# The recurrence's triangles inverted by 32x32 blocks, and attention units spread over its steps

## The chip, the core and the metric

One core of a Trainium2 chip runs the whole kernel. The metric is the time of one execution on the device, in microseconds. The core has a matrix engine (TensorE, PE below; its weight loads are listed apart as PEld), VectorE (DVE), ScalarE (ACT), GpSimd (POOL) and SyncE (SP), which issues DMAs. Every engine runs its own list of instructions in order and waits for the others on semaphores. The lists are fetched from memory by DMA; their packets have a queue of their own in the profile.

## The reference

One step of a decoder layer, for a prompt of 512 tokens and 8 sampled sequences of 8 tokens each with a past of 1,024 cached keys: project the normed input, mix it in four groups of four heads (RWKV7, FoX, MoBA, stick-breaking), project back, then a normed MLP. The part that changes is the RWKV7 recurrence:

```python
def step(s, inp):
    r_t, w_t, k_t, v_t, kk_t, a_t = inp
    sa = jnp.einsum('bhij,bhj->bhi', s, -kk_t)
    s = (s * w_t[:, :, None, :] + sa[..., None] * (kk_t * a_t)[:, :, None, :]
         + v_t[..., None] * k_t[:, :, None, :])
    return s, jnp.einsum('bhij,bhj->bhi', s, r_t)
...
s_fin, y = lax.scan(step, s0.astype(f32), xs)
```

The other three groups are softmax or stick-breaking attention over the prompt (24 attention units here, with the prompt's own keys) and over the cached keys.

## The kernel before

The 576 new tokens (512 of the prompt, 64 sampled) are cut into nine chunks of 64. Inside a chunk the recurrence is solved at once: with L the strictly lower triangular 64x64 matrix of products of kk and kk a, the kernel needs the inverse of (1 + L) for each chunk and head. It builds it by doubling: X starts as the inverse of the diagonal's 2x2 blocks, and level lev (0 to 4) joins neighbouring blocks of size 2, 4, 8, 16 and 32: W = (L masked to this level) X, dX = X W, X = X - dX. The transpose XT (slot 8) goes along through dXT. All this is done with full 64x64 products.

The recurrence is a list STEPS of (kind, a), a = 0 or 1 for a pair of heads: LT and L (both triangles), ArbT, LkT, ArkT, Vt, KQt, BEt, KEt, then W, dX, dXT by level, then T1, HT, H, G, MT, N, seq1 to seq7 (the state from chunk to chunk), U, Y, SS, GM, GV. They are numbered R0 to R74. Each of LT to G is 18 products of 64x64 (nine chunks, two heads on the two halves of the partitions), all issued from line 1154 in `per_chunk`. A product in fp32 is two matmul instructions, each with its weight load, so a step is 36 loads and 36 matmuls. The result stands in PSUM, 128 partitions by 576 columns, in one of two buffers used in turn; `begin` has TensorE wait until the step two back is evicted, and until its operands are there. ScalarE evicts the kinds in BY_ACT (`take_product`, line 1908), VectorE the others (`rwkv_steps`, lines 2507 to 2537, with a mask multiplied or a subtraction done on the way).

What stands between two steps is written out by hand in PLAN: TensorE, ScalarE and VectorE all walk the same list ORDER. In it As u, Ap u and Ay u are the three parts of attention unit u on TensorE (scores, lines 1277; probabilities turned, line 1294; times V, line 1303), with the softmax or stick-breaking work on the other engines between them; units 0 to 5 cover the first 128 queries and 128 keys, 6 to 11 the second 128 queries and 256 keys, and so on. The piece with number u of As, Ap and Ay runs the stage of unit u, u-2 and u-2. K u turns and scores cached keys (lines 1317, 1325 and 1339: 128x128 turns, then products with 32-column weights on four parts of the array in turn), V u multiplies cached values, G ends the recurrence, L loads forget gates. Before R23 the steps follow each other, with L at L_AT.

rc holds masks (lines 60 to 110 of the constants), loaded by two DMAs on SyncE's queue: first part in_rc 16, second in_rc 32. GpSimd stores the new keys and values (kv) during the steps.

Of the kernel before, what the change touches and what calls it, by code (L numbers as in the profile page):

```python
# [33 lines left out]
T = SEQ + NS  # L34
# [8 lines left out]
CH = 64  # L43
# [23 lines left out]
R_SU, R_IU, R_LEV, R_L1, R_L1T, R_BM = 0, 576, 1152, 1472, 1536, 1600  # L67
# [11 lines left out]
def constants():  # L79
# [17 lines left out]
    for n, m in enumerate((2, 4, 8, 16, 32)):  # L97
        rc[:, R_LEV + n * 64:R_LEV + (n + 1) * 64] = level(t[None, :], q[:, None], m)
    rc[:, R_L1:R_L1 + 64] = level(q[:, None], t[None, :], 1)
    rc[:, R_L1T:R_L1T + 64] = level(t[None, :], q[:, None], 1)  # L100
# [20 lines left out]
def build(nc, d, o):  # L121

    ctx = ExitStack()
    with ctx:
# [63 lines left out]
        def chunked(n):  # L188
            return slot(n).rearrange("p a (c s) -> p a c s", s=CH)

# [176 lines left out]
        ltm_ready = sem("ltm_ready")  # L367
        masked_ready = sem("masked_ready")
# [290 lines left out]
        BY_ACT.update({f"W{lev}": (5, 1.0) for lev in range(5)})  # L659

# [35 lines left out]
        L_AT = (2, 6, 10)  # L696
        AFTER = {n: [("L", L_AT.index(n))] for n in L_AT}
        ORDER = []
        for n in range(A_FROM):
            ORDER += [("R", n)] + AFTER.get(n, [])  # L700
        PLAN = """
            As0 R23 R24 R25 Ap0 Ay0 As1 R26 R27 Ap1 R28 R29 Ay1 As2 R30 R31 R32 R33 R34 R35 R36 R37 R38 Ap2 Ay2 R39
            R40 As3 R41 R42 Ap3 R43 R44 Ay3 R45 R46 As4 R47 R48 Ap4 R49 Ay4 As5 R50 R51 R52 R53 R54 R55 R56 R57 Ap5
            R58 R59 R60 R61 R62 R63 R64 Ay5 As6 R65 Ap6 Ay6 As7 B0 R66 Ap7 R67 R68 B1 Ay7 R69 R70 As8 R71 R72 Ap8
            As9 Ay8 R73 R74 G0 G1 Ap9 G2 K0 G3 K1 G4 Ay9 K2 As10 K3 Ap10 K4 Ay10 As11 K5 Ap11 K6 Ay11 K7 As12 K8
            Ap12 K9 K10 K11 Ay12 K12 K13 As13 K14 Ap13 K15 Ay13 As14 K16 K17 K18 Ap14 K19 Ay14 K20 K21 K22 As15 K23
            K24 N0 S0 Ap15 Ay15 P0 M0 K25 As16 K26 K27 Ap16 K28 Ay16 Q0 K29 K30 X0 As17 K31
            Ap17 K32 Ay17 K33 X1 As18 K34 Ap18 K35 Ay18 X2 K36 As19 V0 K37 K38 V1 Ap19 K39 Ay19 K40 As20 K41 V2 V3 Ap20 K42 Ay20 As21 V4 K43
            Ap21 K44 V5 Ay21 K45 K46 As22 V6 K47 N1 Ap22 V7 Ay22 S1 As23 V8 Ap23 V9 Ay23 P1 As24 Ap24 F0 O0 T0 M1 X3
            Ay24 As25 Q1 Ap25 O1 X4 X5 Ay25 O2 V10 O3 V11 V12 V13 V14 V15 V16 V17 V18 V19 F1 T1  # L710
# [231 lines left out]
        def _(pe):  # L942
# [217 lines left out]

            def rwkv_products():

                for kind, A, B in (("LT", 8, 1), ("L", 1, 8), ("ArbT", 8, 4), ("LkT", 3, 1), ("ArkT", 3, 4),
                                   ("Vt", 6, eye), ("KQt", 1, eye), ("BEt", 9, eye), ("KEt", 5, eye)):
# [525 lines left out]
        def _(act):  # L1690
# [166 lines left out]
            for t in range(4):  # L1857
                take(5, t)
            act.wait_ge(logf_in, 1)
            nc.scalar.preload_act_table_set("natural_log_exp_and_others")  # L1860
# [346 lines left out]
        def _(dve):  # L2207
# [291 lines left out]
            id64 = cst[:, K_ID64:K_ID64 + 64].unsqueeze(1).to_broadcast([128, NCH, 64])  # L2499
            def rwkv_steps():  # L2500

                for kind, dst, m in (("LT", 0, R_SU), ("L", 2, None), ("ArbT", 11, R_IU), ("LkT", 7, R_SU), ("ArkT", 12, R_IU)):
                    for a in range(2):
                        src = take(kind, a)
                        if kind == "L":
                            dve.wait_ge(in_rc, 32)
                            link(tt(chunked(dst)[:, a], r3(src), mask64(R_L1), MUL))
                            tt(chunked(dst)[:, a], id64, chunked(dst)[:, a], SUB).then_inc(c_ev, 1)  # L2508
                            yield
                        else:  # L2510
                            tt(slot(dst)[:, a, :], src, rc[:, m:m + T], MUL).then_inc(c_ev, 1)
                            yield
                def level_mask(lev, a):
                    tt(chunked(3)[:, a], chunked(0)[:, a], mask64(R_LEV + 64 * lev), MUL).then_inc(ltm_ready, 1)

                for kind, dst in (("Vt", 14), ("KQt", 15), ("BEt", 17), ("KEt", 18)):
                    for a in range(2):
                        if kind in ("Vt", "KQt"):
                            if kind == "Vt":
                                link(tt(chunked(8)[:, a], chunked(0)[:, a], mask64(R_L1T), MUL))  # L2520
                                link(tt(chunked(8)[:, a], id64, chunked(8)[:, a], SUB))
                            else:
                                level_mask(0, a)
                        yield
                dve.wait_ge(c_ev, AT["KEt", 1] + 1 - by_act(AT["KEt", 1] + 1))
                for lev in range(5):
                    for a in range(2):
                        if lev < 4:
# [692 lines left out]
```

## Time and profile before

| | us |
|---|---|
| median of three runs | 936.02 (933.02 to 936.2) |
| span of the profiled execution | 930.9 |
| time around the span (median less span) | 5.1 |
| first recurrence product (R0) | 205.8 |
| HT (R48) starts | 267.3 |
| sequential state steps start, end | 283.7, 290.7 |
| K0 starts | about 320 |
| As12 (behind K7) starts | 339.8 |

The span is that of one execution taken by the hardware profiler; the times of the runs are of unprofiled ones. The profiled execution has no time of its own apart from the span; its time is taken as the median, so 5.1 us lie around the span. The rows give microseconds, counted from the span's start, unless marked ns.

### The profile page before, as it was taken

How to read it: one execution, taken by the hardware profiler on the slowest of the kernel's cores; microseconds unless marked ns; L12 is line 12 of the kernel's file. 1: busy time of each engine (PE TensorE's matmuls, PEld its weight loads, DVE VectorE, ACT ScalarE, POOL GpSimd, SP SyncE). 2: the span in 40 equal slices, each digit the busy share in tenths (PEclk: the TensorE clock that was granted, in tenths of full speed). 3: DMA queues.
4: the chain of work that ended last, by engine and by line, in shares of the span. 5: the costliest groups of instructions: out<-in, count | busy, mean ns of one | idle time of the engine just before them, and what ended most of it. 6: DMA issues, size and time to landing. Idle time of an engine off the chain costs nothing.

```text
span 930.9 us, 21268 instructions
## 1 busy us (share of the span) xinstructions
PE 894.3 (96%) x8588; PEld 769.5 (83%) x8588; DVE 640.8 (69%) x1083; ACT 452.0 (49%) x771; POOL 63.0 (7%) x95
## 2 busy tenths in 40 slices
PE   6999999998999999979999999999999999999998
PEld 5999899998887667756655789978998899889986
DVE  5563377647756763665664662789988988988796
ACT  6422636313241466775562533453574456535751
POOL 0000112114500000000000000100110000000000
PEclk9999999999999999989999999999999999999999
DMA  8542787861200687648997704886889532443343
GB/s 270 181 137 69 160 203 198 241 133 62 83 6 3 216 283 241 221 141 282 305 397 259 246 20 137 206 271 183 244 211 258 191 91 93 179 136 92 132 143 144
DMA packets 73163, 164.47 MB, mean 177 GB/s; under 512 B 5918, under 2 KB 32126, under 8 KB 70890
## 3 DMA queue, kind: packets, MB, share of 16 engines
q1 hardware_dynamic: 59370, 124.26, 38.9%
q0 software_dynamic: 13696, 38.85, 17.9%
q8 instruction: 68, 1.11, 0.5%
q14 instruction: 29, 0.24, 0.1%
HBM read 156.55 MB, written 40.10 MB: 211 GB/s over the span
## 4 chain that ended last, share of the span: by engine, by line
PE 82%; DVE 11%; ACT 3%; DMA 2%; issue 2%; DVEq 0%; ACTq 0%; SPq 0%
PE PS L962 16%; PE PS L964 15%; PE PS L963 15%; PE PS L1154 7%; PE PS L1317 4%; PE PS L1389 2%; PE PS L1339 2%; PE PS L995 2%; PE PS L1277 2%; PE PS L1303 2%; PE PS L1425 2%; DVE WL L2924 1%; PE PS L1294 1%; PE PS L1629 1%; PE PS L1630 1%
## 5 line engine op out<-in xcount | busy, mean ns | idle before, releaser
L963 PE MATMUL PS<-WL,U 128*128 128x512 f32 x224 | 87.6, 391 | 0.0
L962 PE MATMUL PS<-WH,U 128*128 128x512 f32 x224 | 87.5, 390 | 0.0
L2037 ACT ACTIVATE WH<-Wraw 128x1024 fp32r<-128x1024 f32 x56 | 57.9, 1056 | 48.9 <-PE PS L964 19.9
L2924 DVE TENSOR_TENSOR WL<-Wraw,WH 128x1024 fp32r<-128x1024 f32 x56 | 66.9, 1219 | 7.9 <-ACT WH L2037 7.9
L1154 PE MATMUL PS<-AR 64*64 64x64 f32 x1912 | 61.6, 219 | 4.0 <-DVE AR L2508 1.4
L1154 PEld LDWEIGHTS PS<-AR 64*64 64x64 f32 x1912 | 58.5, 135 | 7.3 <-issue 4.2
L962 PE MATMUL PS<-WR,HR 128*128 128x384 f32 (+1 forms) x184 | 63.7, 346 | 0.8 <-issue 0.8
L962 PE MATMUL PS<-h2H,WH 128*128 128x288 f32 x208 | 61.4, 295 | 1.2 <-DVE rc L3046 1.2
L1317 PE MATMUL PS<-cst,AR 128*128 128x128 f32 x384 | 54.7, 286 | 7.6 <-ACT W L1915 7.6
L963 PE MATMUL PS<-h2L,WH 128*128 128x288 f32 x208 | 61.2, 294 | 0.0
L964 PE MATMUL PS<-h2H,WL 128*128 128x288 f32 x208 | 61.2, 294 | 0.0
L1317 PEld LDWEIGHTS PS<-cst,AR 128*128 128x128 f32 x384 | 43.3, 145 | 20.5 <-ACT W L1915 10.7
L964 PE MATMUL PS<-WH,U 128*128 128x512 f32 x152 | 59.2, 389 | 0.0
L962 PE MATMUL PS<-TF,WH 128*128 128x288 f32 x192 | 56.8, 296 | 0.0
L963 PE MATMUL PS<-TF,WH 128*128 128x288 f32 x192 | 56.7, 295 | 0.0
L964 PE MATMUL PS<-TF,WL 128*128 128x288 f32 x192 | 56.5, 294 | 0.0
L963 PE MATMUL PS<-WR,HR 128*128 128x384 f32 (+1 forms) x160 | 53.9, 337 | 0.0
L1915 ACT ACTIVATE W<-PS 128x512 f32<-128x512 f32 x72 | 40.0, 594 | 25.7 <-PE PS L1317 25.7
L962 PEld LDWEIGHTS PS<-WH,U 128*128 128x128 f32 x224 | 42.1, 188 | 9.4 <-DVE VQ L3050 0.4
L963 PEld LDWEIGHTS PS<-WL,U 128*128 128x128 f32 x224 | 42.0, 188 | 9.0
L964 PE MATMUL PS<-WR,VQL 128*128 128x384 f32 (+1 forms) x138 | 46.3, 335 | 0.0
L2097 ACT ACTIVATE WH<-Wraw 128x1024 fp32r<-128x1024 f32 x24 | 25.4, 1060 | 31.4 <-DVE Wraw L2990 16.2
(436 smaller groups left out, 2310.4 us busy)
## 6 DMA issues: line engine op xcount, KB each, us to landing
AR<-in_cache_kv SPq DMA_DIRECT2D x120, 384.0 KB, 4.8
tau<-in_w_mlp_down POOLq DMA_DIRECT2D x24, 1024.0 KB, 9.0
Wraw<-tau SPq DMA_DIRECT2D x16, 1024.0 KB, 4.8
Wraw<-in_w_mlp_up SPq DMA_DIRECT2D x14, 1024.0 KB, 5.6
Wraw<-in_w_mlp_down SPq DMA_DIRECT2D x12, 1024.0 KB, 5.1
W<-in_w_in SPq DMA_DIRECT2D x6, 1536.0 KB, 9.6
QK<-in_cache_kv SPq DMA_DIRECT2D x8, 384.0 KB, 5.4
AR<-in_x_prompt SPq DMA_DIRECT2D x4, 512.0 KB, 6.8
```

The source lines that it names most:

```text
L962: mm(out, lH, rH, start=start, stop=False, skip_group_check=skip)
L963: mm(out, lH, rL, start=False, stop=False, skip_group_check=skip)
L964: return mm(out, lL, rH, start=False, stop=stop, skip_group_check=skip)
L995: last = mm(PS[rows, bank:bank + c1 - c0], hs[k // 6][:, k % 6, :], piece_raw(i)[:, k, c0:c1], start=(k == 0), stop=(k == KT - 1), skip_gr ...
L1154: last = mm(PS[h, base + c * CH:base + (c + 1) * CH], chunked(A)[h, a, c, :], B(h, a, c) if callable(B) else chunked(B)[h, a, c, :], start ...
L1277: last = mm(PS[:, (4 + h) * 512:(4 + h) * 512 + nk], qT[rows, j, qt * 128:(qt + 1) * 128], kT[rows, j, 0:nk], start=True, stop=True)
L1303: last = mm(PS[64 * h:64 * h + 64, turned_at(u) * 512:turned_at(u) * 512 + 128], V(k, (2 * j + h) * HD, HD), PTp[:, h, k * 128:(k + 1) * 1 ...
L1317: last = turn(PS[:, bank * 512 + bb * 128:bank * 512 + (bb + 1) * 128], page_home("K", s)[:, bb, (m % 6) * 128:(m % 6 + 1) * 128], ident)
L1915: f(KTr[m % 4], PS[:, KEY_BANK[m] * 512:(KEY_BANK[m] + 1) * 512], ACT.Copy).then_inc(kt_ev, 1)
L2037: f(piece_half(WH, r, d, h), piece_half(Wraw, r, d, h), ACT.Copy).then_inc(w_hi, 1)
L2097: ins = f(form_pair(WH, p, r), raw_pair(i, p), ACT.Copy)
L2924: tt(piece_half(WL, r, d, h), piece_half(Wraw, r, d, h), piece_half(WH, r, d, h).bitcast(F32), SUB).then_inc(w_lo, 1)
```

## The change

Each triangle of 64x64 is treated as two diagonal 32x32 blocks and one crossing block. LT and L are computed by halves: only the diagonal blocks, 32 columns each, and for LT the crossing block in 32x32 pieces. Levels 0 to 3 act on the diagonal blocks alone, as 32x32x32 products on the four diagonal tiles of the array in turn (`per_block`); levels 2 and 3 leave out the ninth chunk (the sampled tokens, in groups of 8). Level 4 becomes W4 and dXT4, 16 products each on the crossing block, with T1 between them. The blocks lie in halves of the slots (`blocks`); VectorE puts the diagonal blocks of XT into slot 8 by eight copies, and ScalarE adds the crossing one. Evictions are 288 or 256 columns wide. Half-size PSUM buffers let `begin` look three steps back instead of two within the levels. LT is evicted by ScalarE in three pieces. Masks move within rc, so that L needs the first part alone. L_AT changes, an activation table is preloaded a little earlier, and the list of items is new up to K8: there are as many steps as before, but the units stand elsewhere. From K8 on the list is the same.

```diff
         STEPS = [(k, a) for k in ("LT", "L", "ArbT", "LkT", "ArkT", "Vt", "KQt", "BEt", "KEt") for a in (0, 1)]
-        for lev in range(5):
-            STEPS += [(f"{k}{lev}", a) for k in (("W", "dX", "dXT") if lev < 4 else ("W", "dXT")) for a in (0, 1)]
-        STEPS += [(k, a) for k in ("T1", "HT", "H", "G", "MT", "N") for a in (0, 1)]
+        for lev in range(4):
+            STEPS += [(f"{k}{lev}", a) for k in ("W", "dX", "dXT") for a in (0, 1)]
+        STEPS += [(k, a) for k in ("W4", "T1", "dXT4", "HT", "H", "G", "MT", "N") for a in (0, 1)]
...
+        BY_ACT.update({"LT": (0, 1.0), "dXT4": (8, -1.0)})
+        HALVED = [f"{k}{lev}" for lev in range(4) for k in ("W", "dX", "dXT")]
+        def level_chunks(lev):
+            return NCH if lev < 2 else NCH - 1
+        def step_at(n):
+            return (n % 2) * 1024 + (n // 2 % 2 * 512 if STEPS[n][0] in HALVED else 0)
+        def step_out(n, chunks=NCH):
+            return PS[:, step_at(n):step_at(n) + chunks * HC].rearrange("p (c s) -> p c s", s=HC)
+        def before_step(n):
+            return n - 3 if all(m < len(STEPS) and STEPS[m][0] in HALVED for m in (n, n - 2, n - 4)) else n - 1
...
-        L_AT = (2, 6, 10)
+        L_AT = (1, 6, 10)
...
         PLAN = """
-            As0 R23 R24 R25 Ap0 Ay0 As1 R26 R27 Ap1 R28 R29 Ay1 As2 R30 R31 R32 R33 R34 R35 R36 R37 R38 Ap2 Ay2 R39
-            R40 As3 R41 R42 Ap3 R43 R44 Ay3 R45 R46 As4 R47 R48 Ap4 R49 Ay4 As5 R50 R51 R52 R53 R54 R55 R56 R57 Ap5
-            R58 R59 R60 R61 R62 R63 R64 Ay5 As6 R65 Ap6 Ay6 As7 B0 R66 Ap7 R67 R68 B1 Ay7 R69 R70 As8 R71 R72 Ap8
-            As9 Ay8 R73 R74 G0 G1 Ap9 G2 K0 G3 K1 G4 Ay9 K2 As10 K3 Ap10 K4 Ay10 As11 K5 Ap11 K6 Ay11 K7 As12 K8
...
+            As0 R23 Ap0 R24 Ay0 R25 As1 R26 Ap1 R27 R28 Ay1 R29 As2 R30 Ap2 R31 R32 Ay2 R33 As3 R34 Ap3 R35 Ay3 R36
+            R37 As4 R38 Ap4 R39 Ay4 R40 R41 As5 R42 Ap5 R43 Ay5 R44 As6 R45 R46 Ap6 R47 Ay6 R48 As7 R49 R50 Ap7 R51
+            Ay7 R52 As8 R53 Ap8 R54 R55 As9 R56 Ay8 R57 Ap9 R58 R59 R60 R61 R62 R63 R64 R65 B0 R66 Ay9 R67 As10 R68 B1
+            Ap10 R69 Ay10 R70 R71 As11 R72 Ap11 R73 Ay11 R74 G0 G1 G2 K0 G3 K1 G4 K2 K3 K4 K5 K6 K7 As12 K8 Ap12 K9
...
-                need = max([AT[x, a] + 1 for x in after] + ([n - 1] if n >= 2 else []), default=0)
+                need = max([AT[x, a] + 1 for x in after] + ([before_step(n)] if n >= 2 else []), default=0)
                 evacuated(pe, need)
-                return (n % 2) * 1024
+                return step_at(n)
...
+            def halves_of(base, a, A, B):
+                for c in range(NCH):
+                    for h in (0, 64):
+                        for b in (0, HC):
+                            last = mm(PS[h + b:h + b + HC, base + c * HC:base + (c + 1) * HC],
+                                      chunked(A)[h:h + 64, a, c, b:b + HC], chunked(B)[h:h + 64, a, c, b:b + HC],
+                                      start=True, stop=True)
+                return last
+            def per_block(base, a, A, B, chunks):
+                for c in range(chunks):
+                    for r in range(0, 128, HC):
+                        last = mm(PS[r:r + HC, base + c * HC:base + (c + 1) * HC], A[r:r + HC, a, c, :], B[r:r + HC, a, c, :],
+                                  start=True, stop=True)
+                return last
...
+                LTm, X, XT, W_ = blocks(3), blocks(2), blocks(2, True), blocks(5)
+                for lev in range(4):
+                    chunks = level_chunks(lev)
                     for a in range(2):
                         base = begin(f"W{lev}", a, "L" if lev == 0 else f"dX{lev - 1}", "KEt")
                         pe.wait_ge(ltm_ready, 2 * lev + a + 1)
-                        per_chunk(base, a, 3, 2).then_inc(c_ps, 1)
+                        per_block(base, a, LTm, X, chunks).then_inc(c_ps, 1)
                         yield
-                    if lev < 4:
-                        for a in range(2):
-                            base = begin(f"dX{lev}", a, f"W{lev}")
-                            per_chunk(base, a, 8, 5).then_inc(c_ps, 1)
-                            yield
+                    for a in range(2):
+                        base = begin(f"dX{lev}", a, f"W{lev}")
+                        per_block(base, a, XT, W_, chunks).then_inc(c_ps, 1)
+                        yield
                     for a in range(2):
                         base = begin(f"dXT{lev}", a, f"W{lev}")
-                        per_chunk(base, a, 5, 8).then_inc(c_ps, 1)
+                        per_block(base, a, W_, XT, chunks).then_inc(c_ps, 1)
                         yield
-                for kind, A, B, after in (("T1", 7, 14, ()), ("HT", 15, 8, ("dXT4",)), ("H", 8, 15, ()), ("G", 8, 9, ("T1",))):
+                for a in range(2):
+                    base = begin("W4", a, "dX3")
+                    for c in range(NCH - 1):
+                        for h in (0, 64):
+                            last = mm(PS[h + HC:h + CH, base + c * HC:base + (c + 1) * HC], blocks(0, True)[h:h + HC, a, c, :],
+                                      X[h:h + HC, a, c, :], start=True, stop=True)
+                    last.then_inc(c_ps, 1)
+                    yield
...
+                for a in range(2):
+                    base = begin("dXT4", a, "W4", "dXT3")
+                    for c in range(NCH - 1):
+                        for h in (0, 64):
+                            last = mm(PS[h:h + HC, base + c * HC:base + (c + 1) * HC], W_[h + HC:h + CH, a, c, :],
+                                      XT[h + HC:h + CH, a, c, :], start=True, stop=True)
+                    last.then_inc(c_ps, 1)
+                    yield
+                for kind, A, B, after in (("HT", 15, 8, ("dXT4",)), ("H", 8, 15, ()), ("G", 8, 9, ("T1",))):
                     for a in range(2):
                         base = begin(kind, a, *after)
+                        if kind == "HT":
+                            pe.wait_ge(xt_ready, a + 1)
                         per_chunk(base, a, A, B).then_inc(c_ps, 1)
...
+                    elif kind == "LT":
+                        f(blocks(0)[:, a], step_out(n), ACT.Copy)
+                        crossing = PS[:, step_at(n) + 512:step_at(n) + 512 + (NCH - 1) * HC].rearrange("p (c s) -> p c s", s=HC)
+                        f(blocks(0, True)[0:HC, a, 0:NCH - 1], crossing[0:HC], ACT.Copy)
+                        f(blocks(0, True)[CH:CH + HC, a, 0:NCH - 1], crossing[CH:CH + HC], ACT.Copy).then_inc(x_ev, 1)
+                    elif kind == "W4":
+                        f(blocks(5)[HC:CH, a, 0:NCH - 1], step_out(n, NCH - 1)[HC:CH], ACT.Copy)
+                        f(blocks(5)[CH + HC:128, a, 0:NCH - 1], step_out(n, NCH - 1)[CH + HC:128], ACT.Copy).then_inc(x_ev, 1)
+                    elif kind == "dXT4":
+                        f(chunked(8)[0:HC, a, 0:NCH - 1, HC:CH], step_out(n, NCH - 1)[0:HC], ACT.Copy, scale=scale)
+                        f(chunked(8)[CH:CH + HC, a, 0:NCH - 1, HC:CH], step_out(n, NCH - 1)[CH:CH + HC], ACT.Copy,
+                          scale=scale).then_inc(x_ev, 1)
+                    elif kind in HALVED:
+                        chunks = level_chunks(int(kind[1:]))
+                        f(blocks(dst)[:, a, 0:chunks], step_out(n, chunks), ACT.Copy, scale=scale).then_inc(x_ev, 1)
...
+                for a in range(2):
+                    dve.wait_ge(c_ps, AT["L", a] + 1)
+                    link(tt(X[:, a], step_out(AT["L", a]), mask32(R_L1), MUL))
+                    tt(X[:, a], mask32(R_ID), X[:, a], SUB).then_inc(c_ev, 1)
+                    yield
...
-                for lev in range(5):
+                for lev in range(4):
+                    chunks = level_chunks(lev)
                     for a in range(2):
-                        if lev < 4:
+                        if lev < 3:
                             dve.wait_ge(c_ps, AT[f"W{lev}", a] + 1)
                             level_mask(lev + 1, a)
                         yield
-                    for k, x in ((("dX", 2), ("dXT", 8)) if lev < 4 else (("dXT", 8),)):
+                    for k, x in (("dX", X), ("dXT", XT)):
                         for a in range(2):
-                            src = take(f"{k}{lev}", a)
-                            if x == 8 and lev < 4 or x == 2:
-                                dve.wait_ge(c_ps, AT[f"dXT{lev}", a] + 1 if x == 8 else AT[f"dX{lev}", a] + 1)
-                            tt(slot(x)[:, a, :], slot(x)[:, a, :], src, SUB).then_inc(c_ev, 1)
+                            n = AT[f"{k}{lev}", a]
+                            dve.wait_ge(c_ps, n + 1)
+                            tt(x[:, a, 0:chunks], x[:, a, 0:chunks], step_out(n, chunks), SUB).then_inc(c_ev, 1)
                             yield
-                dve.wait_ge(c_ev, AT["dXT4", 1] + 1 - by_act(AT["dXT4", 1] + 1))
-                for kind in ("T1", "HT", "H", "G"):
+                dve.wait_ge(c_ev, AT["dXT3", 1] + 1 - by_act(AT["dXT3", 1] + 1))
+                for a in range(2):
+                    for r in range(0, 128, HC):
+                        ins = copy(chunked(8)[r:r + HC, a, :, r % CH:r % CH + HC], XT[r:r + HC, a])
+                    ins.then_inc(xt_ready, 1)
+                    yield
```

## Rows read from the trace of the kernel before

**Rows 1.** The page, first lines: engines' busy us (share), instructions.

```profile
span 930.9 us, 21268 instructions
PE 894.3 (96%) x8588; PEld 769.5 (83%) x8588; DVE 640.8 (69%) x1083; ACT 452.0 (49%) x771; POOL 63.0 (7%) x95
```

**Rows 2.** Windows: length, PE, PEld, DVE, ACT, POOL busy (count), PE clock, DMA, GB/s.

```profile
205.80:267.32 61.52, 56.80 (x1731) 53.72 (x1731) 41.63 (x85) 17.25 (x38) 24.43 (x44) 1.00 0.24 74
319.53:339.77 20.24, 17.74 (x227) 13.44 (x227) 16.75 (x37) 15.86 (x34) 1.11 (x2) 1.00 0.60 213
...
205.80:233.88 28.08, 25.21 (x804) 24.32 (x805) 19.27 (x31) 8.23 (x13) 12.04 (x24) 1.00 0.29 90
...
233.88:252.02 18.14, 16.71 (x505) 15.86 (x505) 13.18 (x33) 4.45 (x12) 12.39 (x21) 1.00 0.33 101
```

**Rows 3.** Groups by line and shape, 205 to 320: busy us, mean ns.

```profile
L1908 ACT ACTIVATE AR<-PS 128x576 f32<-128x576 f32 x22 | 14.3, 650 | 46.3 <-PE PS L1154 46.2
L2537 DVE TENSOR_TENSOR AR<-AR,PS 128x576 f32<-128x576 f32 x18 | 13.6, 756 | 9.0 <-PE PS L1154 8.9
...
L2642 DVE TENSOR_TENSOR W<-PS,VQ 128x256 f32<-128x256 f32 x2 | 0.8, 425 | 0.0
```

**Rows 4.** Chain of waits, two recurrence steps: start, us, engine, line.

```profile
256.83 2.24 PE PS L1154 x72
```

**Rows 5.** Timeline of PE: start, length until the last one's end, count.

```profile
302.14 0.75 PE L1233 MATMUL PS<-AR,VQ 64*64 64x8 f32 x11
...
327.42 0.30 PE L1339 MATMUL PS<-W,rc 128*32 128x128 f32 x1
...
327.42 0.32 PE L1339 MATMUL PS<-W,rc 128*32 128x128 f32 x4
```

**Rows 6.** The page, DMA queue of instructions: packets, MB, share of 16 engines.

```profile
q8 instruction: 68, 1.11, 0.5%
```

**Rows 7.** Chain of waits: the two gaps called issue.

```profile
233.50 0.39 issue
...
250.98 1.04 issue
```

**Rows 8.** DMA, windows 231.72:232.70, 249.76:250.72, 254.1:255.6, 257.89:261.33, in order.

```profile
q8 instruction: 1, 0.02, 6.0%
...
q0 software_dynamic: 86, 0.28, 85.7%
q8 instruction: 1, 0.02, 6.1%
...
q8 instruction: 1, 0.02, 4.9%
...
q8 instruction: 2, 0.03, 4.2%
```

**Rows 9.** Chain of waits: pieces of units, first 128 queries, then second.

```profile
259.07 0.42 PE PS L1277 x4
...
264.35 0.37 PE PS L1303 x4
...
315.25 0.44 PE PS L1294 x4
315.69 0.63 PE PS L1277 x4
316.32 0.61 PE PS L1303 x8
```

**Rows 10.** DMA, window 207.0:209.7: the masks' load.

```profile
q1 hardware_dynamic: 357, 0.94, 93.9%
```

**Rows 11.** Chain of waits: cached keys turned and scored.

```profile
324.23 1.02 PE PS L1317 x8
325.26 0.57 PE PS L1339 x16
```

**Rows 12.** Windows: a gap among the cached keys, and behind it.

```profile
336.64:338.38 1.74, 0.00 (x1) 0.00 (x0) 1.44 (x3) 1.71 (x5) 0.00 (x0) 1.00 0.97 369
340.08:343.49 3.41, 3.41 (x24) 2.04 (x24) 2.15 (x8) 1.00 (x2) 0.00 (x0) 0.50 0.90 295
```

More of the change, by code:

```diff
@@ L96, in level @@
         return (a // (2 * m) == b // (2 * m)) & (a // m % 2 == 1) & (b // m % 2 == 0)
[L97 to L100, printed above, removed]
+    w, j = p % HC, np.arange(HC)
+    for n, m in enumerate((2, 4, 8, 16)):
+        rc[:, R_LEV + n * HC:R_LEV + (n + 1) * HC] = level(j[None, :], w[:, None], m)
+    rc[:, R_L1:R_L1 + HC] = level(w[:, None], j[None, :], 1)
+    rc[:, R_L1T:R_L1T + HC] = level(j[None, :], w[:, None], 1)
+    rc[:, R_ID:R_ID + HC] = (w[:, None] == j[None, :])
     for b in range(DB):
@@ L189, in chunked, with blocks @@
             return slot(n).rearrange("p a (c s) -> p a c s", s=CH)
+        def blocks(n, second=False):
+            return slot(n)[:, :, T // 2 * second:T // 2 * (second + 1)].rearrange("p a (c s) -> p a c s", s=HC)
         ARf = AR[:, :, :].rearrange("p a c -> p (a c)")
@@ L1159, in eye @@
                 return cst[h, K_ID:K_ID + 128][:, h]
-            def rwkv_products():
-                for kind, A, B in (("LT", 8, 1), ("L", 1, 8), ("ArbT", 8, 4), ("LkT", 3, 1), ("ArkT", 3, 4),
+            def halves_of(base, a, A, B):
[12 more added lines that the diff above has]
+                return last
+            def rwkv_products():
+                for a in range(2):
+                    base = begin("LT", a)
+                    halves_of(base, a, 8, 1)
+                    for c in range(NCH - 1):
+                        for h in (0, 64):
+                            last = mm(PS[h:h + HC, base + 512 + c * HC:base + 512 + (c + 1) * HC],
+                                      chunked(8)[h:h + 64, a, c, 0:HC], chunked(1)[h:h + 64, a, c, HC:CH], start=True, stop=True)
+                    last.then_inc(c_ps, 1)
+                    yield
+                for a in range(2):
+                    base = begin("L", a)
+                    halves_of(base, a, 1, 8).then_inc(c_ps, 1)
+                    yield
+                for kind, A, B in (("ArbT", 8, 4), ("LkT", 3, 1), ("ArkT", 3, 4),
                                    ("Vt", 6, eye), ("KQt", 1, eye), ("BEt", 9, eye), ("KEt", 5, eye)):
@@ new lines, in rwkv_products @@
+                for a in range(2):
+                    base = begin("T1", a)
+                    per_chunk(base, a, 7, 14).then_inc(c_ps, 1)
+                    yield
+                for a in range(2):
+                    base = begin("dXT4", a, "W4", "dXT3")
+                    for c in range(NCH - 1):
+                        for h in (0, 64):
+                            last = mm(PS[h:h + HC, base + c * HC:base + (c + 1) * HC], W_[h + HC:h + CH, a, c, :],
+                                      XT[h + HC:h + CH, a, c, :], start=True, stop=True)
+                    last.then_inc(c_ps, 1)
+                    yield
@@ L2497, in mask64, with mask32 @@
                 return rc[:, c0:c0 + 64].unsqueeze(1).to_broadcast([128, n, 64])
-            id64 = cst[:, K_ID64:K_ID64 + 64].unsqueeze(1).to_broadcast([128, NCH, 64])
+            def mask32(c0, n=NCH):
+                return rc[:, c0:c0 + HC].unsqueeze(1).to_broadcast([128, n, HC])
             def rwkv_steps():
-                for kind, dst, m in (("LT", 0, R_SU), ("L", 2, None), ("ArbT", 11, R_IU), ("LkT", 7, R_SU), ("ArkT", 12, R_IU)):
+                X, XT = blocks(2), blocks(2, True)
+                for a in range(2):
+                    yield
+                for a in range(2):
+                    dve.wait_ge(c_ps, AT["L", a] + 1)
+                    link(tt(X[:, a], step_out(AT["L", a]), mask32(R_L1), MUL))
+                    tt(X[:, a], mask32(R_ID), X[:, a], SUB).then_inc(c_ev, 1)
+                    yield
+                for kind, dst, m in (("ArbT", 11, R_IU), ("LkT", 7, R_SU), ("ArkT", 12, R_IU)):
@@ L2503, in rwkv_steps @@
                     for a in range(2):
                         src = take(kind, a)
-                        if kind == "L":
+                        if (kind, a) == ("ArbT", 0):
                             dve.wait_ge(in_rc, 32)
[L2507 to L2512, printed above, removed]
+                        tt(slot(dst)[:, a, :], src, rc[:, m:m + T], MUL).then_inc(c_ev, 1)
@@ L2513, in level_mask @@
+                        yield
                 def level_mask(lev, a):
-                    tt(chunked(3)[:, a], chunked(0)[:, a], mask64(R_LEV + 64 * lev), MUL).then_inc(ltm_ready, 1)
-                for kind, dst in (("Vt", 14), ("KQt", 15), ("BEt", 17), ("KEt", 18)):
+                    chunks = level_chunks(lev)
+                    tt(blocks(3)[:, a, 0:chunks], blocks(0)[:, a, 0:chunks], mask32(R_LEV + HC * lev, chunks),
+                       MUL).then_inc(ltm_ready, 1)
+                for kind in ("Vt", "KQt", "BEt", "KEt"):
@@ L2517, in rwkv_steps @@
                     for a in range(2):
[L2518 to L2523, printed above, removed]
+                        if kind == "Vt":
+                            evacuated(dve, AT["LT", a] + 1)
+                            link(tt(XT[:, a], blocks(0)[:, a], mask32(R_L1T), MUL))
+                            link(tt(XT[:, a], mask32(R_ID), XT[:, a], SUB))
+                        elif kind == "KQt":
+                            level_mask(0, a)
+                        elif kind == "BEt":
+                            link(nc.vector.memset(chunked(8)[:, a, :, 0:HC], 0.0))
+                            link(nc.vector.memset(chunked(8)[:, a, NCH - 1, HC:CH], 0.0))
@@ L2524, in rwkv_steps @@
                         yield
                 dve.wait_ge(c_ev, AT["KEt", 1] + 1 - by_act(AT["KEt", 1] + 1))
-                for lev in range(5):
+                for lev in range(4):
+                    chunks = level_chunks(lev)
                     for a in range(2):
-                        if lev < 4:
+                        if lev < 3:
                             dve.wait_ge(c_ps, AT[f"W{lev}", a] + 1)
```

22 lines of the change are left out of this document (15 added, 7 removed).

## Prediction

> **What bounds the kernel now.** I read the page first for what is busy: TensorE 96% of the span [rows 1], and in the chain that ended last nearly all pieces are its own. So a change is priced on TensorE's own list, and what VectorE and ScalarE save counts only where TensorE waits for them. Second, the table by stage [rows 2]: from the start of the recurrence's products (205.80) to its step HT (267.32) TensorE is busy 56.80 of 61.52 us, so at most 4.72 us of waiting can be filled there; in 319.53 to 339.77, where the first cached keys are turned, 17.74 of 20.24. Third, the groups by line, for the price of an eviction: a product of 576 columns costs ScalarE 650 ns and VectorE 756, one of 256 columns 425 [rows 3].
>
> Fourth, what one small matmul costs. A step of 18 products 64x64 is 36 matmul records, each with its weight load; two such steps, 72 records, take 2.24 us with their start [rows 4], 29.2 ns per load and matmul in the steady run. Two things about that pace matter. Matmuls of 8 columns on one 64x64 tile in a row run 11 in 0.75 us [rows 5], up to 68 ns each, whereas two tiles in turn with 64 columns make two in 58. So a small product is set by how quickly one tile can follow itself, hardly by its columns. And where four 32-column tiles are in turn, four matmuls lie inside 0.32 us where one alone takes 0.30 [rows 5]: they start some 7 ns apart. Bursts may start that close; what a long run can keep up is another question.
>
> Fifth, the instruction queue, which decides that. The page has 68 packets on it [rows 6], against 2 x 8,588 matmuls and loads [rows 1]: some 253 instructions per packet of 16 KB (I read: pages of 256). TensorE has two gaps put down to "issue", 0.39 us at 233.50 and 1.04 at 250.98 [rows 7]. Between their ends lie 505 matmuls and 505 loads [rows 2], four pages less the semaphore instructions that the row doesn't count. Just ahead of each gap's end an instruction packet moved: at 231.73, 6.0% of 16 engines over 0.98 us, so 0.94 us long, and at 249.77, beside queue 0's kv stores [rows 8]. Both gaps end 1.2 to 1.3 us after the packet. So TensorE ran out of instructions twice, and with only one page in hand, for a packet late by a microsecond or two was enough. The next packet started 1.4 us after the first gap and 2.2 after the second, at 254.19 [rows 8]. Round of one page when starved: 1.4 + 0.9 + 1.2 = 3.5 us in quiet, 2.2 + 1.2 + 1.2 = 4.6 beside other transfers. The shortest spacing of two packets in the whole trace is 3.42 us, in the window of 3.44 that holds two [rows 8]. I take 3.4 us per 256 instructions, 26.6 ns per load and matmul. At 29.2 ns a page lasts 3.74 us: today the fetch is just hidden.
>
> The Trainium skill speaks against this: Runtime: NRT & Kernel Launch, section Instruction fetch mechanics, says that the sequencer fetches the next 16 KiB block while it works on the current one, so that fetching is hidden, because dispatch is slower than the fill. The two gaps disagree, at a pace of 14.6 ns per instruction. By the rule the sum would have no fetch term and come out as the second rival below.
>
> **The change part by part.**
>
> *More, smaller instructions.* Counted from the diff: 32 steps of 36 pairs of load and matmul (LT, L, levels 0 to 4) = 1,152 pairs become LT 2 x 104, L 2 x 72, levels 0 and 1 twelve steps of 72, levels 2 and 3 twelve of 64, W4 and dXT4 four of 32 = 2,112. That is 960 pairs or 1,920 instructions more, 7.5 pages.
>
> *Units moved ahead of HT.* Before R48 stand two more As, three more Ap and three more Ay: 138 instructions. By the pieces in the chain (As 0.42, or 0.63 from unit 6 on; Ay 0.37, and Ap taken like it [rows 9]) 3.3 us, and 8 x 0.14 us for changing over from the recurrence's matmuls (an estimate from the same 2.24 us: 72 x 29.2 ns is 2.10) = 4.4 us.
>
> *When HT starts.* From 205.80 to HT there are 3,462 matmuls and loads [rows 2]; with 1,920 + 138 and about 1% semaphores, 5,570. Counting pages back from the gap at 233.50 (1,609 instructions after 205.80, twelve semaphores, five pages: 341), the first 341 are at hand; the page after them comes with the packet at 209.74, which waits behind the masks' load, when queue 1 keeps the engines 94% busy [rows 10], and is usable at 211.9. What is left, 5,230 instructions, is 20.4 pages x 3.4 = 69.4 us; three of them late at 4.6 instead of 3.4 (the two late ones above and one more in the kv stores) give 3.5. HT at 211.9 + 69.4 + 3.5 = 284.8 instead of 267.3: **+17.5**. The moved units hide in those waits, and so do the evictions at half width, whose cover is the same fetch; without it they'd be bound by 0.45 us per step, under the 1.05 of a step now.
>
> Bounds of this term: if the fetch never binds, and a pair still costs one tile 58 ns, four tiles in turn make it 14.6; the steps take 1,984 x 14.6 + 128 x 29.2 = 32.7 us against 33.6, and with the units' 4.4 and 1.5 for the page at 211.9 HT moves by +5.0. If a round is 2.5 us instead of 3.4 (below the shortest spacing seen, not excluded, since no page was ever asked for faster), 20.4 x 0.9 = 18 us fall away and that bound holds as well. At the other end 29.2 ns per pair as today: 2,112 x 29.2 = 61.7, +28.1.
>
> *Small things.* LT's eviction goes to ScalarE in three pieces (about 1.3 us a step), LT is off VectorE, L no longer waits for the second half of the masks, eight small copies and T1 stand between W4 and HT: all ScalarE or VectorE work of under 2 us per step, covered by the fetch; if that cover is gone, T1's 1.05 us covers the copies. I take 0, at most +1.
>
> *HT to the end of the recurrence's chain* (R48 on): eight pieces instead of four; 4.1 us against 1.5 by the pieces' prices, the second 128 queries' Ap at 0.44 and Ay at 0.61 [rows 9], + 4 x 0.14, less little waiting filled: **+3.0**.
>
> *R65 to R74*: seven pieces, 4.0 us, instead of eleven, 5.4, and 4 x 0.14 less: **-2.0**.
>
> *K0 to K7*: no pieces instead of eight. Without one, a K takes 1.02 + 0.57 [rows 11], some with 0.2 more: 8 x 1.70 = 13.6 us in place of 20.24. The gap of 1.74 us with TensorE idle at 336.64 goes too, and I expect that the 3.41 us at half the clock after it [rows 12] go, worth 1.7: 20.24 + 1.7 - 13.6 = **-8.3** (-6.6 if the clock falls elsewhere). From K8 on the lists agree: nothing.
>
> **Sum.** The profiled execution's span is 930.9; the median of the runs is 936.0, so 5.1 lie around it. 936.0 + 17.5 + 3.0 - 2.0 - 8.3 = 946.2: **946 us**. Its own range, with rounds of 3.0 to 3.7 us (-8, +6) and the clock, is 938 to 955.
>
> **Rivals.**
>
> *No fetch limit, four blocks overlap at 14.6 ns per pair.* 936.0 + 5.0 + 3.0 - 2.0 - 8.3 = 933.7, about no change. For it: pages have never been asked for faster, so the round may overlap; against it the two gaps. 18%.
>
> *The blocks cost half as much again, faster.* If 32 rows halve a tile's round, a pair costs 7.3 ns, the steps 16 us instead of 33.6; the evictions and the page at 211.9 then bind, HT moves by about -6, and the whole is 936.0 - 6 + 3.0 - 2.0 - 8.3 = 923. For it: the starts 7 ns apart [rows 5]. Against: up to 68 ns for 8 columns. It decides if a round of the fetch is below 2.0 us. 10%.
>
> *Every instruction keeps today's 14.6 ns*, whichever tile it goes to: HT +28.1, sum 936.0 + 28.1 + 3.0 - 2.0 - 8.3 = 957; with a page late here and there 959. For it: no longer run in the trace is faster than today's products; against it only short bursts. The Trainium skill has a rule of this kind (TensorE: Matmul & The Clock Gate, section Wait — 56ns, not 53.3ns?: start to start not under about 25 ns however few the columns); by it 2,112 matmuls would take at least 53 us, an estimate, and the sum would be 948. The four starts in 0.32 us disagree with it for different tiles. 13%.
>
> *The fetch limits, and TensorE, idle in each page, drops to its lower clock* (1.2 GHz) as it did after the gap at 336.64 [rows 12]: with a quarter of the 51 us from HT to K8 at half the clock, 946 + 51/8 = 952. 7%.
>
> **Chances.** Forecast 52%, the rivals as above. Faster by over 0.5% (under 931.3; half a per cent is about what a measurement of this kernel can tell): the second rival 10, a third of the first 6, a tail of the forecast 4: 20%. Within: 17%. Slower: 63%. The range runs from 926 (leaves out the second rival and a little) to 960.
>
> **What would show it.** Right: the instruction queue has 75 to 76 packets; in the level steps the matmuls come in bursts of some 250 instructions with starts a few ns apart, and gaps of 1 to 2 us called "issue", each ending 1.2 us after an instruction packet; packets 3.4 to 3.5 us apart from W0 to dXT4; HT near 285, the first K near 338, K8 some 13.6 us later. Wrong: level steps of 1.05 us without such gaps (then 934), or of 0.5 (923); evenly spaced pairs of 29 ns would be the third rival. The prediction fails if pages can be had faster than 3.4 us when asked for, which no row of before tests.

## The result, and the profile after

The changed kernel takes 961.44 us (median of four runs, 961.01 to 963.42) against 936.11 (933.02 to 936.55): ratio 1.0278, 95% interval 1.026 to 1.0297. It is slower, as forecast, but by 25 us and not by 10, and just outside the stated range. The first lines of its page, the granted clock in 40 slices, the instruction queue and the costliest new group, in answer to [rows 1] and [rows 6]:

```profile
span 960.0 us, 23197 instructions
PE 903.8 (94%) x9548; PEld 773.6 (81%) x9548; DVE 631.5 (66%) x1089; ACT 453.4 (47%) x783; POOL 61.9 (6%) x95
...
PEclk9999999998558989999999999999999999999999
...
q8 instruction: 76, 1.25, 0.5%
...
L1201 PE MATMUL PS<-AR 32*32 32x32 f32 x1632 | 27.3, 235 | 18.0 <-issue 18.0
```

960 more matmuls and as many loads, eight more instruction packets, and 18.0 us of "issue" ahead of the 32x32 products, a kind of idle time of which the kernel before has 1.4 us in its products. Two more gaps, 5.0 us together, stand ahead of products of LT and L. In the chain of waits, these two and then the first of the levels, which start at 236.2:

```profile
207.94 3.84 issue
...
214.62 1.16 issue
...
236.23 0.72 PE PS L1201 x52
236.95 2.85 issue
239.80 2.01 PE PS L1201 x126
241.80 1.70 issue
243.50 1.92 PE PS L1201 x127
245.42 1.77 issue
```

The gaps end multiples of 256 apart in TensorE's list (within one instruction): counted from its start, with semaphore instructions, they end ahead of instructions 3,009, 3,265, 4,545, 4,801, 5,057, 5,314 and so on, the two of [rows 7] at 4,289 and 5,313. Between two of the gaps shown stand 126 or 127 matmuls with their loads, one page, done in 2 us; the rest of the time TensorE has none. The windows by stage (columns as in [rows 2]): from R0 to W0, to T1, to HT, to the first sequential step, to As12:

```profile
206.07:236.16 30.09, 23.77 (x862) 22.69 (x863) 12.89 (x29) 8.11 (x16) 12.70 (x26) 0.83 0.23 70
236.16:291.99 55.83, 37.84 (x1746) 31.43 (x1744) 21.28 (x72) 11.49 (x40) 11.61 (x19) 0.52 0.15 44
291.99:299.48 7.49, 7.15 (x148) 5.82 (x147) 6.90 (x22) 4.36 (x13) 0.00 (x0) 0.69 0.02 4
299.48:317.47 17.99, 17.52 (x444) 15.07 (x442) 11.23 (x38) 9.57 (x27) 0.00 (x0) 1.00 0.01 3
317.47:371.72 54.25, 49.91 (x708) 37.73 (x709) 31.71 (x64) 18.28 (x36) 1.11 (x2) 0.94 0.42 139
```

The last column but two is the granted clock: 0.52 in the levels, so nearly all at the lower level (1.2 GHz), where the kernel before has 1.00 [rows 2]. Against the same stages of before:

| stage | before | after | difference |
|---|---|---|---|
| R0 to W0 | 23.00 | 30.09 | +7.1 |
| W0 to T1 | 36.94 | 55.83 | +18.9 |
| T1 to HT | 2.67 | 7.49 | +4.8 |
| HT to the sequential steps | 15.24 | 17.99 | +2.7 |
| sequential steps to As12 | 56.11 | 54.25 | -1.9 |
| As12 to the end | 591.1 | 588.3 | -2.8 |

T1 stands ahead of dXT4 in the changed kernel and behind it before, so the second and the third line are better read as one: 39.6 us before, 63.3 after, +23.7. Of the +7.1 in the first line, 5.0 are the two gaps ahead of LT and L.

One slip in what stands ahead: HT (R48) of the kernel before starts at 268.4; 267.3 is the second step of T1. The span grew by 29.1 us, the medians by 25.3. Around the span of after lie 1.7 us (961.7 of its own time less 960.0), and 1.6 to 1.8 in every execution of the other kernels that lists both, not the 5.1 that I added. So the execution profiled before took some 932.6 us (an estimate, 930.9 and 1.7): near the lowest of its times (933.02), not the median.

### The profile page after: what moved, and what is told of

It is laid out like the page before. It is cut to its first block, busy times and chain, and to the rows that moved or that the text cites. A ratio compares the mean times of both kernels' runs of the same rounds, so it can differ in the third digit from the quotient of the medians.

```text
span 960.0 us, 23197 instructions
## 1 busy us (share of the span) xinstructions
PE 903.8 (94%) x9548; PEld 773.6 (81%) x9548; DVE 631.5 (66%) x1089; ACT 453.4 (47%) x783; POOL 61.9 (6%) x95
## 4 chain that ended last, share of the span: by engine, by line
PE 82%; DVE 11%; issue 4%; ACT 2%; DMA 0%; DVEq 0%; ACTq 0%
PE PS L988 15%; PE PS L989 15%; PE PS L990 15%; PE PS L1180 4%; PE PS L1397 4%; PE PS L1201 3%; PE PS L1469 2%; PE PS L1419 2%; PE PS L1357 2%; PE PS L1021 2%; PE PS L1383 2%; DVE WL L3038 1%; PE PS L1505 1%; PE PS L1374 1%; PE PS L1710 1%
## 5 line engine op out<-in xcount | busy, mean ns | idle before, releaser
L988 PE MATMUL PS<-WH,U 128*128 128x512 f32 x224 | 87.7, 392 | 0.0
L1397 PE MATMUL PS<-cst,AR 128*128 128x128 f32 x384 | 54.7, 287 | 6.0 <-ACT W L2010 5.1
L1201 PE MATMUL PS<-AR 32*32 32x32 f32 x1632 | 27.3, 235 | 18.0 <-issue 18.0
L1201 PEld LDWEIGHTS PS<-AR 32*32 32x32 f32 x1632 | 24.2, 148 | 22.7 <-issue 20.3
L2192 ACT ACTIVATE WH<-Wraw 128x1024 fp32r<-128x1024 f32 x24 | 25.4, 1059 | 31.5 <-DVE Wraw L3104 21.6
```

What stands on the lines that cost most here:

```text
L988: mm(out, lH, rH, start=start, stop=False, skip_group_check=skip)
L1201: last = mm(PS[r:r + HC, base + c * HC:base + (c + 1) * HC], A[r:r + HC, a, c, :], B[r:r + HC, a, c, :], start=True, stop=True)
L1397: last = turn(PS[:, bank * 512 + bb * 128:bank * 512 + (bb + 1) * 128], page_home("K", s)[:, bb, (m % 6) * 128:(m % 6 + 1) * 128], ident)
L2192: ins = f(form_pair(WH, p, r), raw_pair(i, p), ACT.Copy)
```

## The experiments

Eleven runs were made, on two chips; each stands against the kernel before as it ran beside it (931.6 us on one chip, 933.1 and 934.0 on the other). The theory: pages of 256 instructions, at 3.4 us or more each, set TensorE's pace. Its rivals: the new list, the lower clock, the pace of small products.

**The list alone.** Old triangles, new list:

```diff
-        L_AT = (2, 6, 10)
+        L_AT = (1, 6, 10)
...
-            As0 R23 R24 R25 Ap0 Ay0 As1 R26 R27 Ap1 R28 R29 Ay1 As2 R30 R31 R32 R33 R34 R35 R36 R37 R38 Ap2 Ay2 R39
+            As0 R23 Ap0 R24 Ay0 R25 As1 R26 Ap1 R27 R28 Ay1 R29 As2 R30 Ap2 R31 R32 Ay2 R33 As3 R34 Ap3 R35 Ay3 R36
```

> The old triangles by 64x64 products with the new list of items and the new places of the forget-gate items. If the loss comes from the number of TensorE's instructions (fetch theory), the list alone costs nothing: HT moves by 0 to +4 us, the stretch behind it by -3 to -6, and the time is 929 to 937 us with TensorE at full clock throughout the recurrence. If the list is what costs (rival: the pieces between the steps delay the recurrence), it is 945 us or more.

Measured: 938.57 us, ratio 1.0073 (1.0049 to 1.0097): 7 us slower, between the two. HT comes 7.2 us later, where I had 0 to 4, and behind the sequential steps only 2.8 us come back up to As12. What takes it there is a wait that I had not priced. Its chain of waits:

```profile
324.92 0.76 DVE AR L2592
...
326.31 0.70 DVE W L2654
...
327.04 0.70 DVE W L2654
...
330.42 0.77 DVE AR L2592
...
331.24 1.24 PE PS L1251 x4
```

Between the group norm's two halves (L2592) VectorE does 4 us of a stick-breaking unit (the scans of L2654), since As11 now stands there in the list; TensorE's product L1251 waits 3.4 us for the second half. The changed kernel has the same wait; in this run and in that one, by the waits of TensorE:

```profile
PE PS L1251 <- DVE AR L2592: 3.4, 1, 3.4
```

```profile
PE PS L1331 <- DVE AR L2706: 3.3, 1, 3.3
```

**The blocks alone.** New triangles, old list from R23 on.

> The new triangles by 32x32 blocks with the old list (only the first forget-gate item stays at its new place). Fetch theory: still 960 to 967 us, since all 1,920 added instructions are there: gaps called issue at page boundaries, 256 instructions apart, 3.5 us or more from page to page, and the lower clock. Rival, the list costs: 940 us or less.

Measured: 960.1 us, ratio 1.0284 (1.0242 to 1.0327), HT at 296.9, 28.5 us later than before. The blocks carry the whole loss; the list's 7 us hardly add to them (HT at 299.5 with both, 2.6 us later and not 7.2). I take it that its pieces fill time in which TensorE has no instructions; no run shows that by itself.

**TensorE kept busy.** Two matmuls of 192 columns ahead of each step of LT, L and levels 0 to 3:

```diff
+            def keep_busy(base):
+                for _ in range(2):
+                    mm(PS[:, base + 304:base + 496], ident, cst[:, 0:192], start=True, stop=True)
...
             def per_block(base, a, A, B, chunks):
+                keep_busy(base)
```

> The changed kernel, with two matmuls of 128x128x192 that nobody reads put ahead of each of the 28 steps LT, L and levels 0 to 3, so that TensorE has work while it waits for its next page (some 220 instructions more). Fetch theory with the clock as a second cost: the clock stays high, pages still come 3.5 to 3.7 us apart, the time falls by 6 to 12 us to 950 to 955. If the lower clock is the main cost (rival), the time falls to 940 us or below. If the clock costs nothing, it rises by the added 3 us to 964.

Measured: 964.52 us, ratio 1.034 (1.0308 to 1.0372), as if the clock cost nothing, and not 950 to 955. W0 to T1 by windows, and a stretch of its timeline:

```profile
237.30:293.71 56.41, 47.90 (x1838) 38.04 (x1837) 20.74 (x71) 10.30 (x37) 11.24 (x18) 0.94 0.14 42
```

```profile
239.60 0.82 PE L1208 MATMUL PS<-AR 32*32 32x32 f32 x72
240.35 0.92 PE L1201 MATMUL PS<-cst 128*128 128x192 f32 x4
241.20 0.38 PE L1208 MATMUL PS<-AR 32*32 32x32 f32 x23
242.37 0.62 PE L1208 MATMUL PS<-AR 32*32 32x32 f32 x49 [0.79 <-issue]
```

The clock is 0.94 in place of 0.52, the stage as long, and the pages as far apart: 14 spacings in 54.7 us, 3.90 us each, against 13 in 51.0, 3.92, in the changed kernel. Its gaps called issue are shorter, 8.5 us in the stage and not 18.0, since the added matmuls stand in them, and the pages come no sooner. So in the starved levels the lower clock goes with TensorE's idle time and costs next to nothing of its own. Outside them it does cost: from ArbT to the end of KEt there are no gaps between pages and nothing was added, and that stretch is 2.4 us longer in the changed kernel, where a quarter of it ran at the lower clock (first row, granted clock 0.87), than here (second row, 1.00):

```profile
216.68:236.16 19.48, 18.34 (x515) 17.72 (x511) 11.66 (x25) 4.55 (x7) 8.32 (x18) 0.87 0.14 42
```

```profile
219.47:236.53 17.06, 16.02 (x519) 15.47 (x511) 11.67 (x25) 4.56 (x7) 7.27 (x15) 1.00 0.13 38
```

The timeline also gives the blocks' own price at full clock: the next group starts 0.75 us after a step of 72 pairs, 10 ns per pair.

**One pass.** The blocks' operands in bfloat16, half the instructions in the same steps:

```diff
-            return slot(n)[:, :, T // 2 * second:T // 2 * (second + 1)].rearrange("p a (c s) -> p a c s", s=HC)
+            return slot(n).bitcast(BF16)[:, :, T // 2 * second:T // 2 * (second + 1)].rearrange("p a (c s) -> p a c s", s=HC)
```

> The changed kernel with the blocks' operands kept in bfloat16, so that a block product is one load and one matmul instead of two of each; list, steps, tiles, waits and evictions stay. This changes the precision of the triangles' inverse. 880 pairs, 1,760 instructions, 6.9 pages fewer. Fetch theory: 6.9 pages x 3.7 us less and most of the lower clock gone: 926 to 938 us. Rivals: only TensorE's work counts, 880 x 7.8 ns = 7 us less, 954 us; the chain of evictions and waits is what binds: 958 to 961 us.

Measured: 936.87 us, ratio 1.0044 (1.0024 to 1.0064), on the chip where the blocks alone took 960.1 in two passes. 69 packets (`q8 instruction: 69` on its page) and W0 to T1 in 31.5 us instead of 55.8; the gaps go on to 255 us, the starved part, and stop where the pieces of units fill a page's time. 880 pairs of work could not have given more than 14 us even at half clock (2.01 us for 126 pairs in the chain above, 16 ns each). Nor did evictions become shorter: VectorE is busy for 630.6 us in place of 631.5, ScalarE for 454.1 in place of 453.4.

**More instructions in the kernel before.**

```diff
+            def more(base):
+                for k in range(15):
+                    r = k % 4 * 32
+                    mm(PS[r:r + 32, base + 800:base + 832], cst[r:r + 32, 0:32], cst[r:r + 32, 0:32], start=True, stop=True)
```

> The kernel before, old triangles and old list, with 15 products of 32x32x32 on constants, read by nobody, added to each of the 32 steps LT, L and levels 0 to 4: the same 960 pairs of load and matmul as the change adds. Fetch theory: a level step has 132 instructions, the 28 level steps 14.4 pages at 3.6 to 3.9 us (the spacing in the changed kernel), 52 to 56 us in place of 40, with some 2 us more in LT and L: 14 to 20 us over the kernel before, with gaps called issue at page boundaries, 256 instructions apart. Rival, only TensorE's own work counts: 960 pairs at 7.8 ns, 7.5 us over it, and no such gaps.

Measured: 955.08 us, ratio 1.0241 (1.0219 to 1.0263), 22 us, above both. Its chain, one level's steps:

```profile
264.52 1.19 PE PS L1154 x36
265.71 0.38 PE PS L1165 x30
266.09 0.61 PE PS L1154 x16
266.70 0.87 issue
267.57 0.80 PE PS L1154 x19
```

The gaps are there (at 5,314, 5,569, 5,825, 6,337 and on), the pages 3.78 us apart. But the 30 added pairs also cost 0.38 us a step, 13 ns each, and the step beside them 1.19 instead of 1.05: 0.5 us x 32 = 17 us of work, and fetch adds the rest. The run supports the gaps; it does not separate work from fetch.

**The products twice.** `for r in (0, 32, 64, 96, 0, 32, 64, 96)` in `per_block`.

> The changed kernel with each block product of levels 0 to 3 issued twice, into the same place: 1,632 pairs of load and matmul more, 3,264 instructions, 12.75 pages. Fetch theory: 12.75 x 3.6 to 3.9 us, 46 to 50 us over the changed kernel, some 1,005 to 1,012. Rival, the pace of the blocks themselves: 1,632 x 7.8 ns at full clock to 15.7 at half, 13 to 26 us over it, 973 to 987.

Measured: 1,005.36 us, ratio 1.0765 (1.0737 to 1.0793), 71.4 us over the kernel before; the changed kernel was 26.7 over it on the same chip (959.82 us, the next run below), so the second product costs 45. Its chain, 60 us into the levels:

```profile
299.28 1.63 PE PS L1201 x106
300.91 0.83 issue
301.74 0.54 PE PS L1201 x20
302.27 0.73 PE PS L1357 x4
303.00 1.53 PE PS L1201 x102
304.54 1.03 issue
```

25 pages in a row take 92.6 us, 3.70 each (3.3 at the least), with a gap ahead of each. This is the fetch measured nearly by itself: 12.75 pages more x 3.70 = 47 us, and 45 came; at the blocks' own pace, even at half the clock, it would have been 26.

**The change again, and small stores.** The changed kernel on the second chip, and with the store of the new values cut to 8 columns of each half:

```diff
-                pool.dma_start(orows("kv", i, AW, 2 * AW).rearrange("n (h c) -> n h c", h=2),
-                               ring[0:nr, :, i, :]).then_inc(stored, 16)
+                pool.dma_start(orows("kv", i, AW, AW + 16).rearrange("n (h c) -> n h c", h=2),
+                               ring[0:nr, :, i, 0:8]).then_inc(stored, 16)
```

> The changed kernel as it is, on the same chip as the others of this call: 25 us over the kernel before, ratio 1.026 to 1.030, and the gaps at the same places in TensorE's list, multiples of 256 apart.

> The changed kernel with the store of the new values cut to 8 columns of each half, so that most of 1.9 MB isn't moved between 245 and 258 us (this leaves that part of an output unwritten). Theory: the two pages that came after 5.1 and 5.3 us there were late because their packets waited behind these stores; they come after 3.5 to 3.7, and the time falls by 3 us against the changed kernel on the same chip. Rival: the pages are late for another reason (the distance to the next request), and the time stays within 1 us.

Measured: 959.82 us, ratio 1.0296 (1.0273 to 1.032), and 960.59, ratio 1.0297 (1.027 to 1.0325). The change repeats on the second chip, with the gaps at the same places (3,009, 3,265, 4,545, 4,801, 5,057, 5,314). The small stores give no gain: my reading of the two late pages was wrong. With queue 0 at 8.5% of the engines instead of 96% a page is still late at the same place, 2.5 us after TensorE entered the page ahead of it (249.80 to 252.26). The windows 247.1 to 250.15 of the changed kernel and 247 to 252.3 of this one:

```profile
q0 software_dynamic: 277, 1.01, 96.4%
```

```profile
q0 software_dynamic: 280, 0.04, 8.5%
```

The two profiles aren't enough to compare single pages either: in the profile of the change again, with the stores in full, the same two pages come after 4.8 and 3.9 us and not after 5.1 and 5.3. What delays those packets is open. GpSimd issues DMAs from 245 to 251 in both; that these, and not their bytes, are the cause wasn't tried.

**Unit 11 later.** The list alone, with its wait taken away:

```diff
-  ... R71 As11 R72 Ap11 R73 Ay11 R74 G0 G1 G2 K0 G3 K1 G4 K2 K3 K4 K5
+  ... R71 R72 R73 R74 G0 G1 G2 K0 G3 As11 K1 G4 K2 Ap11 K3 Ay11 K4 K5
```

> The old triangles with the new list, as in the run of the list alone, but with the three pieces of unit 11 moved from R72 to R74 into K1 to K3. There VectorE did 4 us of a stick-breaking unit's work ahead of the group norm's second step, and TensorE waited 3.4 us for that step and dropped to its lower clock for 3.4 us. Theory: wait and dip go, the list's cost of 7 us against the kernel before falls to 1 to 4. Rival: VectorE's work only moves and delays the cached keys by as much: it stays at 6 to 8.

Measured: 939.71 us, ratio 1.0066 (1.0046 to 1.0086): no gain, the rival. PE's waits from 205 to 375:

```profile
PE PS L1317 <- ACT W L1915: 3.8, 1, 3.8
PE PS L1154 <- DVE AR L2537: 2.4, 2, 2.0
...
PE PS L1251 <- DVE AR L2592: 0.9, 2, 0.7
```

The 3.4 us at the group norm became 0.7, and 3.8 appeared at the cached keys: VectorE's scans only moved, now ahead of the exponentials in front of ScalarE's eviction of a K.

**The ninth chunk left out, and with another order.** In the kernel before:

```diff
-                        per_chunk(base, a, 3, 2).then_inc(c_ps, 1)
+                        per_chunk(base, a, 3, 2, range(level_chunks(lev))).then_inc(c_ps, 1)
```

(so too for dX and dXT, and for the evictions' width); the second kernel has `As11 K5 K6 K7 Ap11 Ay11` besides.

> The kernel before, with the one part of the change that takes work away without adding instructions: levels 2 to 4 leave out the ninth chunk, whose groups of 8 tokens have nothing there to join. 64 pairs of load and matmul fewer, evictions of 512 columns in place of 576. By TensorE's own time, 64 x 29.2 ns = 1.9 us less than the kernel before, ratio 0.998. Rival: the late pages or VectorE's waits set these steps, and it is the same within 0.5 us.

> A try at a faster kernel: the kernel before with the ninth chunk left out at levels 2 to 4 and, in the old list, the turned probabilities beside K5 and K6 moved behind K7, so that ScalarE evicts the turned keys of K5 to K7 before it does unit 11's exponentials. If the gap of 1.74 us and the 3.4 us at half the clock behind it go: 1.9 + 1.7 + 1.7 = 5 us under the kernel before, ratio 0.995. Rival: the wait only moves to the next piece, and it is 1 to 2 us under it, as with the ninth chunk alone.

Measured: 931.83 us, ratio 0.9993 (0.9979 to 1.0006), and 931.87, ratio 0.9981 (0.9967 to 0.9994). The first can't be told from no change. The second is the only kernel here clear of the kernel before on the fast side, by 2 us and not by 5; that its order gives anything beyond the ninth chunk isn't shown, since the two take 931.83 and 931.87. Its gap among the cached keys fell to 0.5 and 0.6 us and no lower clock follows, but in the profiled execution two late pages cost TensorE 2.7 us of "issue".

## Why the prediction was right in what binds and wrong in its size

**Right: what binds.** The fetch of TensorE's instructions, read from two gaps of 1.4 us together, is the cause, and the count came out: 76 packets (75 to 76 were forecast), 5,555 instructions between R0 and HT (5,570 by my sum), the first page usable at 211.8 (211.9). That the sum is so close is luck: the 3,462 leave out T1's second step, 72 instructions, and the pieces moved ahead of HT have 52 instructions and not 138. Half the instructions took the loss away but for 5 us, twice the products added 45. By the Trainium skill's rule that fetching is hidden (Runtime: NRT & Kernel Launch, Instruction fetch mechanics) the sum had no fetch term, 934 or 923 by the two rivals without one; the 18.0 us of gaps disagree with it.

**Mis-sized: "20.4 pages x 3.4 = 69.4", +17.5.** 20.4 pages took 87.7 us, from 211.8 to 299.5. Three things were off. First, only the level steps are starved. The four pages of ArbT to KEt took 18.5 us, 4.6 each, and the 2.4 of W4, T1 and dXT4 12.7: there the products, half of them at the lower clock, and the pieces take longer than a fetch. I put the fetch's price on pages that their own work sets; a page costs the larger of the two. That is 9.5 us of the 14.7 missing at HT. Part of it is the lower clock, which the sum had at nothing: 2.4 us up to the end of KEt (the rows under the run with TensorE kept busy), and some 1.3 from T1 to HT, 7.5 us here with a granted clock of 0.69 against 6.2 at full clock in the change run again:

```profile
287.97:294.18 6.21, 5.14 (x148) 4.15 (x146) 5.90 (x16) 4.94 (x13) 0.00 (x0) 1.00 0.02 5
```

Second, the 13 pages of the levels took 52.5 us, 4.0 each: 3.3 to 4.1 for most (1.0 to 1.9 from entering a page to its successor's packet, 0.9 to 1.3 for the packet, 1.3 to 1.6 until TensorE runs), three over 5. The first of these three fell beside a load on queue 1 (85.9% of the engines from 234.3 to 237.3); why the other two came late is open. 3.4 was the shortest spacing seen, and so a floor; I used it as a mean. Third, 0.6 us in the first page. Against the 18.4 of all three I had 3.5 for late pages.

**Wrong: "K0 to K7, -8.3" and "R65 to R74, -2.0".** Together the stages from the sequential steps to As12 gave 1.9 back, not 10.3. The eight K's without pieces took 16.1 us, some 3 of them lost to the lower clock (granted 0.82 over them), which I expected to go and which came after another gap; and a wait of 3.3 us for VectorE took the place of the gap of 1.74 [rows 12]. The list's text shows TensorE's pieces only; the units' work on VectorE, 4 us for a stick-breaking unit, moves with them, and I priced none of it. In the list alone the same oversight shows once more: 2.0 us ahead of T1's second step, TensorE waiting for VectorE's step on dXT4, which has 4 us of the units' work ahead of it.

**Right in size: HT to the sequential steps**, +2.7 for +3.0.

**The rivals.** The pace of 14.6 ns per instruction is out, 10 ns per pair at full clock. So is four blocks in turn at 14.6 ns per pair: the blocks are as fast as the second rival had them, or nearly (10 for 7.3), and it didn't matter, since the fetch came first. The lower clock came, ahead of HT and for nearly all of the levels, where the rival had it for a quarter of 51 us behind HT; in the starved levels it was a companion, around them a cost. Two of the prices don't follow from my own terms: the third rival's +28.1 leaves out the 4.4 and 1.5 that the first rival has, and HT (284.8) to K8 (13.6 us behind a first K near 338) is some 67 us, not 51. Neither changes which rival is out.

**The base.** With 1.7 instead of 5.1 us around the span the sum would have been 943. The misses: +13.3 from R0 to HT (30.8 for 17.5), -0.3 from HT to the sequential steps, +8.4 from there to As12, -2.8 behind As12, +0.3 in the start, -3.4 in the base: 15.5, from 946.2 to the profiled execution's 961.7.

## What to carry to other kernels

Before cutting products into smaller ones, count instructions: where TensorE ran 256 of them in less time than one fetch, here 3.7 us on the mean of 25 pages, it waited for the rest, whatever the arithmetic saved. Price each page at the larger of its fetch and its own work, and look for gaps called "issue" that lie a multiple of 256 instructions apart. When a list of pieces is rearranged on a busy engine, price what moves with them on the other engines: taken away in one place, the same wait stood in another.

## What the runs showed of the hardware that was not expected

Blocks of 32x32 on the four diagonal tiles in turn cost 10 ns per load and matmul at full clock, where two 64x64 tiles in turn cost 29; the Trainium skill's floor of about 25 ns from start to start (TensorE: Matmul & The Clock Gate, Wait — 56ns, not 53.3ns?) does not hold from tile to tile. The levels ran at a granted clock of 0.52, and at 0.94 with matmuls added ahead of their steps; the pages came 3.92 and 3.90 us apart. And an instruction packet came 2.5 us after TensorE had entered the page ahead of it, where 1.0 to 1.9 is usual, with queue 0 at 8.5% of the DMA engines.
